# The state-space branch issued inside the sample attention stage of a hybrid decoder step, with the sample's value products in 64-row halves

## The reference

```
z = rms_norm(x, g_mix) @ w_in                       # u, q, k/v of three kinds, gates
ssm: x_t = lambda x_(t-1) + B u_t;  y = gelu(C x_t + D u_t)      # 32 groups, scan over time
     a, b = split(y @ w_glu);  ssm_out = (a * sigmoid(b)) @ w_ssm_proj
attention: o = g0 * compressed + g1 * selected blocks + g2 * window
x = x + (sigmoid(g_s) * ssm_out + sigmoid(g_a) * (o @ w_attn_proj)) @ w_out
y = x + hierarchical mixture of experts(rms_norm(x, g_ffn))       # 32 experts, top 2
```

## Time and profile before

| | us |
|---|---|
| median of three runs | 1394.59 (1392.9 to 1445.29) |
| the profiled execution's own time | 1392.34 |
| its span from first to last instruction | 1390.7 |

### The profile page before, as it was taken

How to read it: one execution, slowest core, us unless ns; L and a number is a source line. 1 busy time by engine, 2 the same in 40 slices (tenths; PEclk the granted TensorE clock), 3 DMA queues, 4 the chain that set the end, 5 groups by cost and what they waited for, 6 DMA issues and landing times. The chain is left out here.

```text
span 1390.7 us, 17123 instructions
## 1 busy us (share of the span) xinstructions
PE 1111.5 (80%) x6170; PEld 703.0 (51%) x6170; DVE 389.9 (28%) x961; ACT 270.3 (19%) x567; POOL 237.4 (17%) x604
## 2 busy tenths in 40 slices
PE   5999997877775877998999965987777777777760
PEld 5999997754344665666774533332222222322220
DVE  4447341657742333131232133000000000000005
ACT  6323222334431122112000110110010000101102
POOL 0008911188404120000000001011000000000010
PEclk9999997668877888557999975999999999999995
DMA  8321342220009530433006023999999999999946
GB/s 339 104 85 62 105 171 80 65 105 1 5 12 305 157 114 21 196 142 121 0 0 264 31 112 124 422 421 422 421 421 422 421 422 421 422 421 422 422 191 219
DMA packets 71241, 299.32 MB, mean 215 GB/s; under 512 B 12070, under 2 KB 30374, under 8 KB 44678
## 3 DMA queue, kind: packets, MB, share of 16 engines
q1 hardware_dynamic: 60734, 274.79, 49.8%
q0 software_dynamic: 9296, 22.71, 4.7%
q10 hardware_dynamic: 1152, 1.05, 0.2%
HBM read 284.27 MB, written 25.58 MB: 223 GB/s over the span
## 5 line engine op out<-in xcount | busy, mean ns | idle before, releaser
L1880 PE MATMUL ps<-arena 128*64 128x512 f32 x1024 | 242.4, 626 | 70.1 <-DMA arena<-in_w_exp 52.3
L346 PE MATMUL ps<-local_project 128*128 128x288 f32 (+4 forms) x1608 | 205.2, 290 | 17.2 <-DVE local_project L485 16.4
L346 PEld LDWEIGHTS ps<-local_project 128*128 128x128 f32 (+1 forms) x1608 | 204.2, 184 | 17.7 <-DVE local_project L485 16.4
L1880 PEld LDWEIGHTS ps<-arena 128*64 128x64 f32 x1024 | 79.4, 143 | 222.3 <-issue 200.2
L1880 PE MATMUL ps<-local_late,arena 128*64 128x512 f32 x512 | 117.7, 603 | 32.6 <-DMA local_late<-in_w_exp 31.3
L1928 DVE SCALAR_TENSOR_TENSOR arena<-arena,ps 128x512 f32<-128x512 f32 x16 | 11.0, 688 | 310.9 <-ACT arena L1912 310.9
L1880 PEld LDWEIGHTS ps<-local_late,arena 128*64 128x64 f32 x512 | 40.2, 138 | 109.2 <-issue 109.2
L1536 PE MATMUL ps<-arena 128*128 128x512 f32 (+1 forms) x160 | 71.3, 606 | 1.4 <-DVE arena L1656 1.4
L1850 POOL TENSOR_TENSOR arena<-arena 1x1 f32<-1x1 f32 x16 | 2.9, 184 | 348.8 <-ACT arena L1920 348.8
L1904 ACT ACTIVATE arena<-ps 128x512 f32<-128x512 f32 x34 | 18.5, 594 | 217.3 <-PE ps L1863 217.3
L1931 DVE SCALAR_TENSOR_TENSOR arena<-arena,ps 128x512 f32<-128x512 f32 x16 | 11.0, 688 | 159.5 <-PE ps L1880 159.5
(11 more groups left out here) (381 smaller groups left out, 1521.0 us busy)
## 6 DMA issues: line engine op xcount, KB each, us to landing
arena<-in_w_exp SPq DMA_DIRECT2D x128, 1024.0 KB, 25.5
local_late<-in_w_exp SPq DMA_DIRECT2D x64, 1024.0 KB, 25.8
arena<-in_w_rest SPq DMA_DIRECT2D x9, 1024.0 KB, 5.7
arena<-in_w_wide SPq DMA_DIRECT2D x6, 1040.0 KB, 4.9
scratch_sig<-arena POOLq DMA_DIRECT2D x16, 288.0 KB, 2.6
arena<-scratch_sig SPq DMA_DIRECT2D x1, 4608.0 KB
arena<-in_x SPq DMA_DIRECT2D x2, 2048.0 KB, 7.9
arena<-in_cache POOLq DMA_DIRECT2D x32, 128.0 KB, 3.7
```

What stands on the lines that cost most here:

```text
L346: mm = pe.matmul(out, stationary(s, k), moving(m, k), start=k == 0 and a == 0, stop=k == KD - 1 and a == 2)
L1880: mm = pe.matmul(c.ps[SLOTS * q:SLOTS * (q + 1), bank, :], tokens[:, k0 + k, SLOTS * q:SLOTS * (q + 1)], raw[p][q][:, k], start=first and ...
```

## The change

**A second stream.** Everything of the state-space branch up to the product with `w_ssm` and its gate moves from `merge` to `sample`. `background()` lists it in 47 numbered steps: 0 to 7 the units `y` of the state-space products, 8 empty, 9 to 12 two turning units `t` each, 13 to 28 the linear and gate halves `g` of the eight GLU units, 29 to 44 the sixteen units `p` of `w_ssm`, 45 and 46 empty. TensorE does step n whole (`back_step(n)`). ScalarE and VectorE do at their point n (`back_out(n)`) what belongs to earlier steps: the square and first products of step n-1 and the tanh and last product of step n-2 for `y`, else the work of step n-1. Steps 0 to 4 stand ahead of period 0 (step 4 behind compression of pair 0). Each period has nine points, k = 0 to 8, and `point(p, k)` = 5 + 9p + k is the step that stands there. On TensorE: 0 after the wide scores, 1 after the compressed keys and values, 2 after the compressed scores, 3 after the head sums, 4 after compression of the next pair, 5 and 6 around the window's value product, 7 and 8 around the selection's. Steps 41 to 46 follow the last period.

```diff
+def background():
+    y = [[("y", n)] for n in range(8)]
+    turn = [[("t", n), ("t", n + 1)] for n in range(0, 8, 2)]
+    glu = [[("g", u, e)] for u in range(8) for e in range(2)]
+    proj = [[("p", u)] for u in range(16)]
+    return y + [[]] + turn + glu + proj + [[], []]
...
+            def back_step(n):
+                for unit in back[n]:
+                    kind, u = unit[0], unit[1]
+                    if kind == "y":
+                        if u >= 2:
+                            pe.wait_ge(y_done, u - 1)
...
+                        if u >= 2:
+                            pe.wait_ge(yt_out, u - 1)
...
+                        if u >= 1 and e == 0:
+                            pe.wait_ge(glu_done, u)
...
+                        if u >= 2:
+                            pe.wait_ge(sp_done, u - 1)
```

**VectorE's order.** The window's additions and maximum now stand first in a period, and the steps of points 3 to 6 stand behind the choice of blocks:

```diff
+                dve.tensor_tensor(S[:, PAST:PAST + 64], c.ps[:, 3, 0:64], nm, ALU.add).then_inc(new_read, 1)
...
+                back_out(point(p, 0))
+                back_out(point(p, 1))
...
                 dve.tensor_scalar(s1[:, 4:5], s1[:, 14:15], -SCALE, None, ALU.mult).then_inc(bias_w, 1)
+                for k in range(3, 7):
+                    back_out(point(p, k))
```

**Scores and value products.** The wide scores alternate between the two sequences. The value products have 64 output rows (both heads of a sequence in one, 128 columns wide) and alternate between the sequences tile by tile; of the 128 columns of a row, the copies into `aT` take only the half of that row's own head:

```diff
-                            for t in tiles:
...
-                                mm = pe.matmul(c.ps[lo:lo + 32, 3 + w, 0:HD], pt[0:r, t * P + lo:t * P + lo + 32], v,
+                    for t in tiles:
+                        a, r = KT[t][1], KT[t][2]
+                        for e in range(2):
+                            lo = 64 * e
...
+                            mm = pe.matmul(c.ps[lo:lo + 64, 5, PV_AT[w]:PV_AT[w] + P], pt[0:r, t * P + lo:t * P + lo + 64], v,
```

**Transfers.** The compression slots have one buffer of their own (`pgc`) in place of two; the window keys and values have one buffer each. The new loads are on SP:

```diff
+            pages(sp, 0, pgc, slice(0, 2), cmp_in, range(PAGES))
+            for p in range(NP):
+                if p:
+                    sp.wait_ge(wide_ps, p)
+                sp.dma_start(wk[:], c.d["win_kT"][:, 2 * p:2 * p + 2]).then_inc(wk_in, 16)
+                if p:
+                    sp.wait_ge(pv_ps, 3 * (p - 1) + 2)
+                sp.dma_start(wv[:], c.d["win_v"][:, 2 * p:2 * p + 2]).then_inc(wv_in, 16)
+                if p == 0:
+                    sp.wait_ge(y_ps, 8)
+                    sp.dma_start(w_glu[:], c.d["w_glu"]).then_inc(wg_in, 16)
+                    sp.dma_start(w_ssm[:], c.d["w_ssm"]).then_inc(ws_in, 16)
+                if p + 1 < NP:
+                    sp.wait_ge(cmp_ps, p + 1)
+                    pages(sp, p + 1, pgc, slice(0, 2), cmp_in)
+                if p == 0:
+                    sp.wait_ge(yt_ps, 8)
+                    sp.dma_start(sig_s[:], c.d["sig"][0:8].rearrange("m p t -> p m t")).then_inc(ss_in, 16)
+            sp.wait_ge(cmp_ps, NP)
+            sp.dma_start(sig_a[:], c.d["sig"][8:16].rearrange("m p t -> p m t")).then_inc(ahead_in, 16)
+            sp.wait_ge(glu_ps, 16)
+            sp.dma_start(w_attn[:], c.d["w_attn"]).then_inc(ahead_in, 16)
+            sp.wait_ge(ahead_in, 32)
```

More of the change, by code:

```diff
@@ new lines, in _ @@
+                for a in range(2):
+                    for e, (row, q) in enumerate(qrow):
+                        pe.matmul(c.ps[row, a, :], q, pg[b][:, e * PAGES + 4 * a:e * PAGES + 4 * a + 4, 0], start=True, stop=True)
+                for row, q in qrow:
+                    mm = pe.matmul(c.ps[row, 3, 0:64], q, kn[:, 0], start=True, stop=True)
+                mm.then_inc(wide_ps, 1)
+                if p:
+                    turned_result(p - 1)
+                back_step(point(p, 0))
@@ L1260, in _ @@
             act.wait_ge(qb_zero, 1)
+            for n in range(START - 1):
+                back_out(n)
             for g in range(2):
@@ L1315, in _, with hidden @@
+            def hidden(p):
                 dve.wait_ge(trail_out, 2 * p + 2)
@@ L1528, in _ @@
+                for k in range(4):
+                    mm = pe.matmul(c.ps[:, 4 + u % 4, 0:HALF], w_attn[:, k, m * P:(m + 1) * P], c.aT[:, k, t],
+                                   start=k == 0, stop=k == 3)
+                mm.then_inc(proj_ps, 1)
             pe.wait_ge(proj_done, 16)
```

607 lines of the change are left out of this document (329 added, 278 removed).

## The result

The changed kernel takes 1381.76 us (median of 4 runs, 1375.69 to 1382.24), beside 1395.82 for the kernel before (1392.9 to 1445.29, 4 runs). The ratio is 0.9898, 95% interval 0.9879 to 0.9916: about 14 us faster, and within the 2% that the prediction calls no change. One run of the kernel before, 1445.29 us, is in a slower state that some executions show and is left out of the ratio. The forecast was 1378 (1354 to 1402). The profiled execution, 1375.69 us with a span of 1374.0, is the shortest of the four by 6 us; the sum had given 1376.4 for it.

What follows compares the result with a forecast made beforehand. Expert stage fixed by weight transfers, so earlier savings move the end one for one; TensorE work fills about 40 us of sample gaps. Sample end 682.0, output projection 716.2, plus 4 for clock: 720.2, 15.9 earlier; 1378 us (1354 to 1402).

Steps and rivals of the forecast that it cites:

- Period 0: Sample stage, first period: 89.8 us of work plus 37.3 of waits from 416.2, ending at 543.3 us.
- the pages: Period 0: cache pages of pair 1 requested behind eight y units and two weight loads; TensorE waits 20.4 us.
- the keys: End of period 0: window keys of pair 1 queue behind gate values, 9.2 us with 4.7 covered: 4.5 wait.
- the value products: Each sample period: 56 alternating double-width products at 0.07 us, 3.9 us in all, 4.3 less; bounds 0.055 and 0.109.
- the waits of turning: Period 0: the turning units wait for ScalarE three times, 3.6 us together.
- Period 1: Second sample period: 20.9 us own work, 19.0 for nine GLU units, 12.1 of waits: 52.0 us.
- The wait at point 3: Period 1: a GLU unit waits for VectorE, whose finishing step stands behind the block selection: 6.1 us.
- The allowance for the clock: Added after the merge: 4 us for low clock after longer waits, from compression at 10.04 against 8.9 us, three periods.
- The high clock in the units: Rival, y units: state-space units run at the high clock, 2.6 us saved each, about 20: 1358 us; chance 0.20.
- The low clock in the interleaved periods: Rival, periods 1 to 3 and tail: clock stays low; at a quarter of the work +29 us, 1407; chance 0.15.
- Without overlap: Rival, value products: halves don't overlap, 0.109 instead of 0.07 us each, 9 us more, 1387; chance 0.08.
- The waits were not shorter: Judges a rival: half the stream's 23 us of waits in periods 1 to 3, pages' wait stays, 1366; chance 0.12.

Runs made afterwards that it cites:

- the experiment that moves the unit: Changed kernel with TensorE's step of point 3 placed behind compression of the next pair instead of ahead of it: 1369.76 us, ratio 0.9838.
- forms alone: Kernel before, no second stream, with only alternating scores and alternating value products of 64 rows and 128 columns: 1380.42 us, ratio 0.9905.
- the units of full rows: Changed kernel, 64-row products in y units replaced by repeats of the 128-row product; one run: a group takes 1.28 us at first, then 0.66.
- the four edits: Changed kernel with pair 1 pages first, window keys before gate values, point 3 step behind compression, fewer row-form changes in y units: 1338.84 us, ratio 0.9588.

## Why the prediction was right, point by point

**Time and its place.** The output projection was put at 720.2 and stands at 721.8; the span's other 2 us are mostly the clock in its last tile, which the sum had left out. That the expert loop only moves held. That the profiled run comes within 0.7 us of the sum's 1376.4 is luck: the other three are 5 to 6 us above it, and the terms below miss by more than that in both directions.

**Period 0** was to end at 543.3 and ends at 543.81, by terms that partly cancel. Right: y0 to y3 27.0 us; y5, y6 and y7 wait 3.15, 2.33 and 2.64 for 3.4, 2.6 and 2.8; the pages, 18.8 for 20.4. From the end of y7 (488.7) the two loads ahead took 1.6 us rather than 0.8, the last page was there 1.8 us after its issue's end rather than 3.2, and the small products cover 1.9 us of it rather than 1.0. Right by luck: the keys, 4.45 for 4.5. From the end of turning they take 10.8 us and not 9.2, and the work that covers them takes 6.4 us and not 4.7, since its value products run at the low clock; the two errors cancel. The 1.7 us to land in that term stands in no row of the trace before. Too high: y4 to y7 at 24.9, since y4 and half of y5 ran at the high clock (22.3). Too low: the value products, 3.9 in the own work, which took 6.8 at the low clock; and the waits of turning, put at 3.6 as three for ScalarE. They were 4.9: 2.44 for VectorE to finish y7, and two for ScalarE, 1.30 and 1.20.

**Period 1**, 52.0 in the sum, is 55.8. The wait at point 3, worked out as 6.1, is 6.19, and the experiment that moves the unit removes it. The other three are 1.76, 1.87 and 1.99 for 2.0 each. The missing 3.8 us is low clock behind a pause: three units behind a wait take 3.41, 4.21 and 3.90 us instead of 2.1, and the first scores of the period 1.7 us more than in the next, less what compression gains (7.63 for 10.0). Periods 2 and 3, each to the end of its last unit, are 46.3 and 33.7 for 46.3 and 32.1, the last four units and the turned result 8.1 for 8.3.

**The allowance for the clock.** The sum had put 4 us for this behind the stage; the periods miss by 5.4 together, so the amount was nearly right and the place not named. The reasoning for it does not hold. It compared a compression of 10.04 us in the middle of a period with one of 8.92 from a cold start, as if 10.04 were free of the low clock. In the kernel before, the compression at the end of period 0 reads

```profile
463.86 7.41 PE L1175 MATMUL ps<-local_sample,arena 128*128 128x128 f32 x64
```

all at clock 1.00, while the one of 10.04 ran at a mean of 0.72. So each of the two middle periods had 2.5 us of slack in its compression, and these 5 us pay for about half of what the six slow units behind waits (some 9 us above their price in the sum) and the scores behind the pause cost.

**The value products.** At the high clock 0.063 us a pass is measured for the 0.07 taken, and that it hangs on the alternation is shown. The upper bound, 0.109 from passes of 512 columns, was too low: unalternated ones of 128 columns take 0.125.

**What the sum did not say.** It gives the new forms 4 x 6.6 = 26 us and the whole change 16, so by its own terms the stream costs 10. The text spoke of work put into gaps of about 40 us and never drew that line. The two experiments show it, at nothing rather than at 10, since without the stream the scores' 2.3 us a period are waited out: forms alone 0.9905, the stream with the old value products 1.001. The stream fills the sample's gaps and pays for it with the pages (18.8), the keys (4.5), the selection (6.2) and the waits for its own earlier units, in a stream of two banks; more banks for it were not tried. With the waits mended and the units placed behind compression, the ratio is 0.9473 and not 0.9905, so a stream does pay. An estimate of 5 to 7 us of that, from 0.15 to 0.21 us for each of 32 changes of form, could be had without a stream as well.

**The rivals.** The high clock in the units came true for one and a half of eight. The Trainium skill ("TensorE: Matmul & The Clock Gate", section "Part 1: The HAM clock gate") has activity raise the clock; y0 to y3, busy for 27 us without a gap at 0.50, disagree, and the units of full rows agree. The low clock in the interleaved periods shows in the unit behind six of the eight waits of periods 1 to 3 (3.3 to 4.2 us for some 2.1), and not in the two whose wait follows soon on compression (582.72 and 630.49, 2.21 us each); it costs 5.4 us net and not 29 or more. Without overlap the value products would have cost 14 us rather than the 9 of that rival. The waits were not shorter.

## What to carry to other kernels

When a second stream is laid into a stage, write down for every wait that it adds what stands behind that wait on the same queue: one transfer request behind an unrelated wait cost 18.8 us here, a unit ahead of the work that used to cover a chain 6.2. Sum the change's parts apart and ask each for its own worth, since two of them can carry a third that brings nothing. Work during which the clock does not rise, as the `y` units here, is cheapest right behind work during which it does.

## What the runs showed of the hardware

- Units that mix 64-row and 128-row products keep the level that they find: 0.50 for 27 us from a low start, 1.00 for 21 us right behind compression, and back to 0.50 at or soon after a wait of 3 us (y5 changes in its third group in the changed kernel, and starts at 0.50 with the four edits).
- With 64-row products alone the clock did not rise in 21 us although TensorE is busy 18.6 of them, the first 9.7 without a gap; with 128-row products of the same 72 weight columns it rose after about 4 us from the first unit, and after about 6 us behind the wait of 4.25. One run of each.
- A change between 128-row and 64-row products costs 0.21 us at the low clock, and about 0.15 at the high one (0.95 us a group with two changes, 0.66 without). The Trainium skill ("TensorEngine Tiling (Array Packing)", section "Key Properties") says that a change of tiling mode drains TensorE; the rows show that each change costs time, and how much, and not by what.
- At the high clock, products with 64 weight columns and 128 moving columns take 0.063 us an instruction alternating between the halves and 0.125 one half at a time: two halves cost as one.
